# Hybrid encoder with a routed expert FFN: places from chosen ranks and filler products in the dispatch, own PSUM banks and ScalarE scaling in the last norm

## The reference

```
h = layer_norm(DEEPNORM_ALPHA * h + mix, ln1_g, ln1_b)
logits = h @ w_router + b_router
top_val, top_idx = top_k(logits, 4); gate = softmax(top_val)
# each expert's tokens are put into blocks, in the order of their rank in the expert
ffn[token] = sum over its 4 experts of gate * (clamped_swiglu(h @ w_e1[e] + b_e1[e]) @ w_e2[e] + b_e2[e])
out = layer_norm(DEEPNORM_ALPHA * h + ffn, ln2_g, ln2_b)
```

## Time and profile before

| | |
|---|---|
| time of three runs | 1649.32, 1646.13, 1648.8 us; median 1648.8 |
| the profiled execution | 1645.04 us, its span 1643.3 us, mean granted clock 0.975 |
| PE busy | 1505.0 us (92%) |
| DVE, ACT, POOL busy | 483.3, 249.8, 230.4 us |
| HBM read and written | 470.12 and 20.97 MB |
| chain that ended last, by engine | PE 72%, DMA 16%, SP's queue 5%, DVE 4% |

### The profile page before, as it was taken

The page is one execution under the profiler, slowest core; times in us unless marked ns, Lnnn a source line. Parts: engine busy times, 40 slices in busy tenths (PEclk is TensorE's granted clock), DMA queues, the critical chain, the costliest instruction groups (busy, mean ns, idle before and its releaser), DMA issues.

```text
span 1643.3 us, 30499 instructions
## 1 busy us (share of the span) xinstructions
PE 1505.0 (92%) x12438; PEld 689.1 (42%) x12439; DVE 483.3 (29%) x933; ACT 249.8 (15%) x302; POOL 230.4 (14%) x301
## 2 busy tenths in 40 slices
PE   7999999999999879999987788998799999999955
PEld 6744444444444534344433333343333444344422
DVE  5034343210004633223223223222322332222226
ACT  4011332110001121111101111011101101111112
POOL 1060000000000001211211211121121112111225
PEclk9999999999999879999999999999999999999987
DMA  5522100163305469999999999999999999999945
GB/s 188 182 77 86 36 1 0 45 191 90 90 1 205 185 258 414 416 414 416 416 414 416 416 414 416 416 416 415 416 416 414 417 416 415 405 374 418 414 187 219
DMA packets 136439, 474.31 MB, mean 289 GB/s; under 512 B 16732, under 2 KB 62532, under 8 KB 103384
## 3 DMA queue, kind: packets, MB, share of 16 engines
q1 hardware_dynamic: 123552, 445.10, 68.8%
q0 software_dynamic: 10896, 16.83, 2.8%
q10 hardware_dynamic: 1960, 11.94, 1.8%
HBM read 470.12 MB, written 20.97 MB: 299 GB/s over the span
## 4 chain that ended last, share of the span: by engine, by line
PE 72%; DMA 16%; SPq 5%; DVE 4%; issue 2%; ACT 1%; POOL 0%; POOLq 0%; DVEq 0%; ACTq 0%
PE ps L1456 26%; DMA big<-in_w_e 14%; PE ps L1489 12%; PE ps L1323 7%; PE ps L1244 5%; PE ps L1353 3%; PE ps L1381 3%; PE ps L1205 3%; PE ps L1337 3%; SPq L477 3%; PE ps L1331 1%; PE ps L1448 1%; SPq L460 1%; PE ps L1482 1%; PE ps L1272 1%
## 5 line engine op out<-in xcount | busy, mean ns | idle before, releaser
L1456 PE MATMUL ps<-big,rest 128*32 128x512 f32 x5040 | 568.9, 604 | 58.2 <-DMA big<-in_w_e 44.1
L1456 PEld LDWEIGHTS ps<-big,rest 128*32 128x32 f32 x5040 | 160.6, 111 | 429.7 <-issue 429.7
L1489 PE MATMUL ps<-big,rest 128*32 128x256 f32 x5120 | 287.9, 381 | 18.7 <-DMA big<-in_w_e 15.5
L1489 PEld LDWEIGHTS ps<-big,rest 128*32 128x32 f32 x5120 | 166.9, 110 | 130.2 <-issue 33.8
L1114 DVE TENSOR_TENSOR rest<-ps,rest 128x1024 f32<-128x1024 f32 x32 | 39.2, 1224 | 594.6 <-PE ps L1456 594.6
L605 POOL DMA_INDIRECT expert_rows<-rest,slot x128 | 127.2, 994 | 56.8 <-issue 29.3
L772 ACT ACTIVATE rest<-ps 128x1024 f32<-128x1024 f32 x33 | 68.6, 2079 | 434.5 <-PE ps L1448 434.5
L776 ACT ACTIVATE rest<-ps 128x1024 f32<-128x1024 f32 x32 | 32.7, 1023 | 426.8 <-PE ps L1482 296.4
L1244 PE MATMUL ps<-big,rest 128*128 128x512 f32 x192 | 82.8, 593 | 2.8 <-ACT big L650 2.8
L1133 DVE TENSOR_TENSOR rest<-ps,rest 128x1024 f32<-128x1024 f32 x32 | 39.2, 1224 | 129.6 <-PE ps L1489 129.6
L590 POOL COPY idx<-P 128x1 uint32 (+1 forms) x33 | 6.1, 183 | 488.5 <-PE ps L1448 469.2
(11 more groups left out here) (225 smaller groups left out, 1192.0 us busy)
## 6 DMA issues: line engine op xcount, KB each, us to landing
big<-in_w_e SPq DMA_DIRECT2D x379, 1024.0 KB
rest<-in_w_in SPq DMA_DIRECT2D x14, 1024.0 KB, 5.1
big<-expert_rows ACTq DMA_DIRECT2D x4, 2048.0 KB, 15.3
gate_area<-in_w_in SPq DMA_DIRECT2D x8, 512.0 KB, 5.3
rest<-in_w_in SPq DMA_DIRECT2D x8, 512.0 KB, 4.5
big<-in_w_out SPq DMA_DIRECT2D x1, 4096.0 KB, 13.1
X<-in_x SPq DMA_DIRECT2D x4, 512.0 KB, 9.4
gate_area<-in_w_branch_mlstm SPq DMA_DIRECT2D x4, 512.0 KB, 6.4
```

Of the source, the lines that this page charges most:

```text
L1456: last = mm(ps[TB * g:TB * (g + 1), b, :], xT[:, k, b, :], w1, start=(k == 0), stop=(k == KD - 1))
L1489: last = mm(ps[TB * g:TB * (g + 1), 4 + b // 2, YW * (b % 2):YW * (b % 2 + 1)], aT[:, b, k % 2, TB * (k // 2):TB * (k // 2 + 1)], W2[:, k ...
```

## The change

It touches two stretches, from the end of W_out to the first expert, and from the last expert to the end.

- `places`: instead of computing places for all 32 experts and picking four at the end (ten wide instructions and two reductions), DVE first picks the four chosen ranks from PSUM (one wide product, one reduction) and computes on 128x4 values. `iota_e` is replaced by the indices of the top four.
- The count reduction on DVE moves ahead of the wait for the slots; the index table is computed straight from PSUM, before `slots_f`; the number of further iterations comes from one conversion instead of a chain of comparisons.
- The first gather reads its indices from the table itself; POOL's copy to `idx` and the wait between go.
- `keep_clock(n)`: n products of the identity with itself into bank 4, whose result nobody reads, at six places on PE: 10, 4, 5, 3 and 14 before the first gather's rows are waited for, 5 before the first expert product.
- The first copy of `xT` is split: ACT takes bank 6, DVE bank 7.
- ACT loads the table with Ln and Exp once ahead of each norm.
- The loads of the combine are eight of 1 MB: rows 0 and 1 of a tile (`yg_front`), then rows 2 and 3 (`yg_back`). POOL takes row 0 in place of row 3. PE takes row 1 for both halves as soon as the front has landed, then rows 2 and 3. Each tile has two PSUM banks of its own.
- Last norm: DVE centres the tile before it refines its own 1/sqrt; ACT scales tile i-1 (`scaled`), DVE adds its bias. Tile 3 is scaled and biased on DVE as before.

```diff
@@ -582,13 +588,16 @@
-def gather(it, first=False):
-    if not first:
-        pool.wait_ge(x_tr, it)
-        own_wait()
+pool.indirect_dma_start(out=xg, out_offset=None, in_=x1_dram,
+                        in_offset=bass.IndirectOffsetOnAxis(ap=idx_table[:, 0:1], axis=0),
+                        bounds_check=S - 1, oob_is_err=False).then_inc(xg_landed, 16)
+def gather(it):
+    pool.wait_ge(x_tr, it)
+    own_wait()
...
-    pool.wait_ge(idx_ready, it + 1)
+    pool.wait_ge(idx_ready, it)
@@ -606,8 +615,6 @@
-gather(0, first=True)
-pool.wait_ge(x_tr, 1)
@@ -620,11 +627,16 @@
+def add_first(i):
+    pool.wait_ge(yg_front[i], 16)
+    row = yg[:, i, 0, :]
+    step(nc.gpsimd.tensor_scalar(row, row, gatew[:, TOPK * i:TOPK * i + 1], None, ALU.mult))
+    nc.gpsimd.tensor_tensor(X0v[:, i, :], X0v[:, i, :], row, ALU.add).then_inc(first_added, 1)
...
-    pool.wait_ge(yg_landed[i], 16)
-    row = yg[:, i, TOPK - 1, :]
-    step(nc.gpsimd.tensor_scalar(row, row, gatew[:, TOPK * i + TOPK - 1:TOPK * (i + 1)], None, ALU.mult))
-    nc.gpsimd.tensor_tensor(X0v[:, i, :], X0v[:, i, :], row, ALU.add).then_inc(fourth_added, 1)
+    add_first(i)
@@ -751,6 +763,7 @@
+act.preload_act_table_set("natural_log_exp_and_others")
@@ -787,10 +800,11 @@
+act.wait_ge(x_tr, 1)
+act.activation(xT[:, 0:KD // 2].rearrange("p c b t -> p c t b"), ps[:, 6, :].rearrange("p (c t b) -> p c t b", t=TB, b=NB), ACT.Copy).then_inc(xT_ready, 1)
...
-take_xT(1)
@@ -813,9 +827,17 @@
-    act.dma_start(yg[:, i], y_dram[P * i:P * (i + 1)]).then_inc(yg_landed[i], 16)
+    act.dma_start(yg[:, i, 0:2], y_dram[P * i:P * (i + 1), 0:2]).then_inc(yg_front[i], 16)
+    act.dma_start(yg[:, i, 2:4], y_dram[P * i:P * (i + 1), 2:4]).then_inc(yg_back[i], 16)
+act.preload_act_table_set("natural_log_exp_and_others")
...
-    rstd(NORM2 + i)
+    s0 = 16 * i
+    act.wait_ge(var2_ready, i + 1)
+    step(act.activation(stat[:, s0 + 14:s0 + 15], stat[:, s0 + 13:s0 + 14], ACT.Ln))
+    act.activation(stat[:, s0 + 14:s0 + 15], stat[:, s0 + 14:s0 + 15], ACT.Exp, scale=-0.5).then_inc(rstd2_ready, 1)
+    if i >= 1:
+        act.wait_ge(centred, i)
+        act.activation(X0v[:, i - 1, :], X0v[:, i - 1, :], ACT.Copy, scale=stat[:, s0 - 2:s0 - 1]).then_inc(scaled, 1)
@@ -1015,19 +1037,19 @@
-    rk, rt, ri = (v[:, E * i:E * (i + 1)] for v in (rank, rtmp, rint))
-    rp = ps[:, 7, E * i:E * (i + 1)]
-    step(nc.vector.tensor_scalar(ri, rp, 1.0 / TB, 0.5 / TB - 0.5, ALU.mult, ALU.add))
-    step(nc.vector.tensor_scalar(rt, ri, float(1 - NB * TB), None, ALU.mult))
-    step(nc.vector.scalar_tensor_tensor(out=rk, in0=rp, scalar=float(NB), in1=rt, op0=ALU.mult, op1=ALU.add))
-    nc.vector.tensor_scalar(ri, rp, 1.0 / CAP, 0.5 / CAP - 0.5, ALU.mult, ALU.add).then_inc(rank_read, 1)
+    rp = ps[:, 7, E * i:E * (i + 1)].rearrange("p (a e) -> p a e", a=1)
+    rk, rt = chosen_rank[:, TOPK * i:TOPK * (i + 1)], rank_tmp[:, TOPK * i:TOPK * (i + 1)]
+    pl, ri, ci = place[:, TOPK * i:TOPK * (i + 1)], rank_int[:, 0:TOPK], rank_int[:, TOPK:2 * TOPK]
+    nc.vector.tensor_tensor(chosen, oh[:, i], rp.broadcast_to([P, TOPK, E]), ALU.mult).then_inc(rank_read, 1)
...
-    step(nc.vector.tensor_copy(rt, ri))
-    step(nc.vector.scalar_tensor_tensor(out=rk, in0=rt, scalar=float(-NB), in1=rk, op0=ALU.mult, op1=ALU.add))
-    step(nc.vector.scalar_tensor_tensor(out=rt, in0=rt, scalar=float(E), in1=iota_e[:], op0=ALU.mult, op1=ALU.add))
-    for what, into in ((rk, place), (rt, itern)):
-        step(nc.vector.tensor_tensor(chosen, oh[:, i], what.rearrange("p (a e) -> p a e", a=1).broadcast_to([P, TOPK, E]), ALU.mult))
-        step(nc.vector.tensor_reduce(into[:, TOPK * i:TOPK * (i + 1)].rearrange("p (k a) -> p k a", a=1), chosen, X_AXIS, ALU.add))
+    step(nc.vector.tensor_reduce(rk.rearrange("p (k a) -> p k a", a=1), chosen, X_AXIS, ALU.add))
+    step(nc.vector.tensor_scalar(ri, rk, 1.0 / TB, 0.5 / TB - 0.5, ALU.mult, ALU.add))
+    step(nc.vector.tensor_scalar(ci, rk, 1.0 / CAP, 0.5 / CAP - 0.5, ALU.mult, ALU.add))
+    step(nc.vector.tensor_scalar(pl, ri, float(1 - NB * TB), None, ALU.mult))
+    step(nc.vector.tensor_copy(rt, ci))
+    step(nc.vector.scalar_tensor_tensor(out=pl, in0=rk, scalar=float(NB), in1=pl, op0=ALU.mult, op1=ALU.add))
+    step(nc.vector.scalar_tensor_tensor(out=itern[:, TOPK * i:TOPK * (i + 1)], in0=rt, scalar=float(E), in1=tf[:, i, :], op0=ALU.mult, op1=ALU.add))
+    step(nc.vector.scalar_tensor_tensor(out=pl, in0=rt, scalar=float(-NB), in1=pl, op0=ALU.mult, op1=ALU.add))
@@ -1059,24 +1081,19 @@
-dve.wait_ge(slots_done, 1)
-nc.vector.tensor_scalar(slots_f, ps[:, 2, 0:N_ITER], float(NO_TOKEN), None, ALU.add).then_inc(slots_read, 1)
-dve.wait_ge(slots_read, 1)
-nc.vector.tensor_scalar(idx_table[:, 0:N_ITER], slots_f, 1.0 / TOPK, -0.375, ALU.mult, ALU.add).then_inc(tables_ready, 1)
...
-step(nc.vector.memset(cnt[:, E + 1:E + 2], 0.0))
-for r in range(1, ROUNDS):
-    step(nc.vector.tensor_scalar(cnt[:, E + 2:E + 3], cnt[:, E:E + 1], float(CAP * r), float(E), ALU.is_gt, ALU.mult))
-    step(nc.vector.tensor_tensor(cnt[:, E + 1:E + 2], cnt[:, E + 1:E + 2], cnt[:, E + 2:E + 3], ALU.add))
+dve.wait_ge(slots_done, 1)
+nc.vector.tensor_scalar(idx_table[:, 0:N_ITER], ps[:, 2, 0:N_ITER], 1.0 / TOPK, NO_TOKEN / TOPK - 0.375, ALU.mult, ALU.add).then_inc(tables_ready, 1)
+nc.vector.tensor_scalar(slots_f, ps[:, 2, 0:N_ITER], float(NO_TOKEN), None, ALU.add).then_inc(slots_read, 1)
+step(nc.vector.tensor_scalar(more_iter[0:1, :], cnt[0:1, E:E + 1], 1.0 / CAP, 0.5 * (CAP - 1) / CAP - 1.0, ALU.mult, ALU.add))
...
-nc.vector.tensor_copy(more_iter[0:1, :], cnt[0:1, E + 1:E + 2]).then_inc(iter_ready, 1)
+nc.vector.tensor_scalar(more_iter[0:1, :], more_iter[0:1, :], float(E), None, ALU.mult).then_inc(iter_ready, 1)
@@ -1087,6 +1104,8 @@
+dve.wait_ge(x_tr, 1)
+nc.vector.tensor_copy(xT[:, KD // 2:KD].rearrange("p c b t -> p c t b"), ps[:, 7, :].rearrange("p (c t b) -> p c t b", t=TB, b=NB)).then_inc(xT_half, 1)
@@ -1154,20 +1173,45 @@
-for i in range(NT):
+def norm_2_statistics(i):
...
-    dve.wait_ge(fourth_added, i + 1)
+    s0 = 16 * i
+    dve.wait_ge(first_added, i + 1)
...
-        nc.vector.tensor_tensor(half, half, ps[:, 2 * (i % 2) + n, :], ALU.add).then_inc(combined_read, 1)
+        nc.vector.tensor_tensor(half, half, ps[:, 2 * i + n, :], ALU.add).then_inc(combined_read, 1)
...
-    close_statistics(NORM2 + i, D // BANK)
+    step(nc.vector.bn_aggr(stat[:, s0 + 12:s0 + 14], stat[:, s0:s0 + 12]))
+    nc.vector.tensor_scalar(stat[:, s0 + 13:s0 + 14], stat[:, s0 + 13:s0 + 14], LN_EPS, None, ALU.add).then_inc(var2_ready, 1)
+    layer_norm_center(NORM2 + i, t)
+def norm_2_root(i):
+    s0 = 16 * i
+    var, y, q = stat[:, s0 + 13:s0 + 14], stat[:, s0 + 14:s0 + 15], stat[:, s0 + 15:s0 + 16]
+    dve.wait_ge(rstd2_ready, i + 1)
+    step(nc.vector.scalar_tensor_tensor(out=q, in0=y, scalar=var, in1=y, op0=ALU.mult, op1=ALU.mult))
+    step(nc.vector.tensor_scalar(q, q, -0.5, 1.5, ALU.mult, ALU.add))
+    nc.vector.tensor_tensor(y, y, q, ALU.mult).then_inc(centred, 1)
+    return y
+def norm_2_bias(i):
+    dve.wait_ge(scaled, i + 1)
+    nc.vector.tensor_tensor(X0v[:, i, :], X0v[:, i, :], bias[:], ALU.add).then_inc(out_ready, 1)
+for i in range(NT):
+    norm_2_statistics(i)
+    y = norm_2_root(i)
...
-        layer_norm_scale(NORM2 + i - 1, X0v[:, i - 1, :], out_ready)
-    layer_norm_center(NORM2 + i, t)
-layer_norm_scale(NORM2 + NT - 1, X0v[:, NT - 1, :], out_ready)
+        norm_2_bias(i - 1)
+dve.wait_ge(centred, NT)
+nc.vector.scalar_tensor_tensor(out=X0v[:, NT - 1, :], in0=X0v[:, NT - 1, :], scalar=y, in1=bias[:],
+                               op0=ALU.mult, op1=ALU.add).then_inc(out_ready, 1)
@@ -1425,14 +1469,25 @@
+def keep_clock(n):
+    for _ in range(n):
+        mm(ps[:, 4, 0:P], ident[:], ident[:], start=True, stop=True)
+pe.wait_ge(wo_read, 2 * NT - 1)
+keep_clock(10)
...
+keep_clock(4)
...
+keep_clock(5)
...
+keep_clock(3)
@@ -1440,6 +1495,7 @@
+keep_clock(14)
@@ -1522,7 +1578,9 @@
+keep_clock(5)
...
+pe.wait_ge(xT_half, 1)
@@ -1550,13 +1608,14 @@
-    pe.wait_ge(yg_landed[i], 16)
+    pe.wait_ge(yg_front[i], 16)
...
-        if i >= 2:
-            pe.wait_ge(combined_read, 2 * (i - 2) + n + 1)
-        for k in range(TOPK - 1):
-            last = mm(ps[:, 2 * (i % 2) + n, :], gate_diag[:, TOPK * i + k, :], yg[:, i, k, BANK * n:BANK * (n + 1)],
-                      start=(k == 0), stop=(k == TOPK - 2))
+        mm(ps[:, 2 * i + n, :], gate_diag[:, TOPK * i + 1, :], yg[:, i, 1, BANK * n:BANK * (n + 1)], start=True, stop=False)
+    pe.wait_ge(yg_back[i], 16)
+    for n in range(D // BANK):
+        for k in range(2, TOPK):
+            last = mm(ps[:, 2 * i + n, :], gate_diag[:, TOPK * i + k, :], yg[:, i, k, BANK * n:BANK * (n + 1)],
+                      start=False, stop=(k == TOPK - 1))
...
```

(3 more changed lines are left out.)

11 lines of the change are left out of this document (8 added, 3 removed).

## The result

Five runs of the changed kernel took 1638.0 to 1640.26 us, median **1639.4**; before, run beside it, takes 1648.8 (1646.13 to 1650.06 in five runs). The ratio is 0.9942, with a 95% interval of 0.9930 to 0.9954. The forecast was 1637.0, range 1631.5 to 1643.0. The profiled execution took 1638.0 (span 1636.3) where that of before took 1645.04 (1643.3).

The account below looks back on a forecast made before the run. The prediction took the loop as bound by the weight stream over DMA, PE close behind, with serial ends. Dispatch 7.7 plus combine 4.1 gave 11.8 us off the median 1648.8: forecast 1637.0, range 1631.5 to 1643.

Parts of the forecast that it names:

- Terms 1 to 5: W_out to last slots: table loads 0.65, logits 1.75, ranks 0.9, places 0.8, last slots 0.4; done 4.5 us earlier.
- Term 6: From last slots to the gather's issue: one DVE instruction and POOL's issue, 0.85 us instead of 2.0, gain 1.1.
- Term 7: First gather meets the weight backlog: issued at 572.85, lands at 578.0, 4.1 us earlier than before.
- The rival in which the gather waits like the store: First gather takes 10.0 us, dispatch gives 2.8, total gain 6.9, time 1641.9; chance 0.10.
- The even share of the Trainium skill: Queues served in turn: the first gather gets half the rate, lands near 577.5, half a microsecond better.
- Term 8: Fillers before the first gather's rows: PE free at 577.3, rows come at 578.0, so they cost nothing.
- Term 9: After the gather: transposes 1.98 to 1.1 us, gain 0.9; split copy with five fillers, gain 1.05.
- Term 10: First expert product: 13.9 us at full clock instead of 15.54, gain 1.6; it ends 7.7 us earlier.
- The rival of the stream that swallows the dispatch: Expert loop: weights' volume alone sets its end, only the combine's 4.1 us stay, time 1644.7; chance 0.12.
- Combine, 4.1: Last expert to end: first half load lands 2.6 us earlier, last tile 0.5 shorter; gain 4.1 us (2.5 to 6).
- a combine without gain: Rival at the combine: POOL and DVE exclude each other, combine gains 0, total 7.7, time 1641.1; chance 0.10.
- the last rival: Dispatch: fillers don't hold the clock and queue at 1.2 GHz; 2.6 to 6.7 us slower, 1653.5; chance 0.08.

Follow-up runs that it names:

- no_fillers: Changed kernel without its 41 filler products on PE; median 1642.3 us, ratio 0.9956 to the kernel before.
- late_slice: Changed kernel with slice 7 of the second expert's weights loaded after slices 0 to 2, not before the gather; median 1637.8 us, ratio 0.9927 to the kernel before.
- tail_fillers: Changed kernel with 75 fillers ahead of the last half of the last expert's second product; median 1651.3 us, ratio 1.0016 to the kernel before.
- all_rests: Changed kernel with the last slice loaded later and fillers at 86 us, before the loop and before the last weights; median 1651.6 us, ratio 1.0016.
- fillers_alone: Kernel before with only the 41 fillers added at the same six places; median 1642.8 us, ratio 0.9966.
- loop_entry_fillers: Changed kernel with ten more fillers ahead of the expert loop; median 1635.8 us, ratio 0.9924 to the kernel before.
- late_slice_fillers: Changed kernel with the last weight slice loaded behind the others and ten fillers ahead of the loop; median 1636.0 us, ratio 0.9919 to the kernel before.
- early_fillers: Changed kernel with 20 fillers in TensorE's rest at 86 us; median 1640.1 us, ratio 0.9944 to the kernel before.
- whole_loads: Changed kernel with one 2 MB combine load per tile again instead of two halves; median 1641.9 us, ratio 0.9960 to the kernel before.
- combine_alone: Kernel before with only the change's combine and last norm; median 1644.3 us, ratio 0.9976.
- dispatch_alone: Kernel before with everything of the change up to the first expert, combine and last norm unchanged; median 1642.6 us, ratio 0.9962.
- scaling_on_dve: Changed kernel with ScalarE's last-norm scaling back on DVE, in one instruction with the bias; median 1638.3 us, ratio 0.9938 to the kernel before.

## Why the prediction was right, and where its sizes were off

**Terms 1 to 5, the slots done 4.5 us earlier.** Measured from W_out's last column it is 4.2: table loads 0.64 for 0.65, logits 1.65 for 1.75, ranks 0.84 for 0.9, places 0.81 for 0.8, last slots 0.3 for 0.4. In no_fillers logits and ranks take 3.63 and 1.92 as before, so those two hang on the fillers.

**Term 6, to the gather, 1.1.** It is 0.6; this step failed. I took 0.5 for what stands between DVE's instruction and the gather, near the 0.3 between two scatters. It is 1.00, of which 0.84 is POOL's issue. The nearer row is that of each gather in the loop, which waits for a copy on its own engine. In after's waits it reads (engine and line waited for, us, times, longest):

```profile
POOL rest L602 <- POOL idx L599: 27.1, 31, 0.9
```

I had read that time as the copy's. But the issue is as long with a copy ahead of it as without one, as the chain of waits of before shows just ahead of the gather:

```profile
577.63 0.85 issue
```

**Term 7, the gather lands 5.15 us after its issue.** 5.12. The reason is right, since late_slice has 3.5 with a slice less. That the number fits so well is luck. The gather was issued 18.0 us behind W_out's last column and not 17.2, so less backlog was left, and it brings 0.22 MB and not 0.5. The same sum with what the trace has, 1.47 MB of weights left at the issue and 0.22 of the gather at 0.42 MB/us, gives 4.0 (an estimate). What the sum left out is that a gather that meets nothing takes 3.5 to 3.6 as well, of which its bytes are 0.5. The slots' shortfall (0.3) and that of term 6 (0.5) came through, so the landing gained 3.3 and not 4.1. The rival in which the gather waits like the store (10 us) is out.

The even share of the Trainium skill (DMA: Bandwidth & Descriptors, "Queues, rings and completion order") would have given about 4.6 with the prediction's bytes. The trace doesn't agree with it: in the first 3.2 us 236 packets of weights moved and none of the gather's, where in before, with no backlog, its first packet came 2.0 us after the issue.

**Term 8, fillers before the rows cost nothing.** PE was free 1.62 us before they came. In late_slice they end just as the rows come, and with one more they would be on the path.

**Term 9, transposes and copy 1.95.** 1.46: the transposes gave 0.89 as said, but from their end to the product it is 1.82 and not 1.35. The two halves of the copy end 1.16 behind the transposes, the five fillers 1.12, and then PE's issue takes 0.70, where the 1.35 left 0.3. How much of that is the fillers' no_fillers tells, whose product starts 1.66 behind the transposes:

```profile
586.77 1.94 PE L1512 MATMUL ps<-big,rest 128*32 128x512 f32 x8 [1.66 <-ACT rest L804]
```

So the fillers cost 0.16 us there, and 0.3 of the shortfall is there without them. Product start: 4.7 earlier for 6.05.

**Term 10, first product 13.9, gain 1.6.** 13.98 and 1.56. Slice 7 didn't delay it.

Dispatch in sum: 6.3 for 7.7. **The loop** passed it on. It ends on the last weights, whose landing moved with the first product's end: 981.8 us behind it before, 982.3 after, 982.9 in late_slice. The 0.6 us that after loses is no loss that one can tell. Without tail_fillers and all_rests, from the end of the first product to DVE's last addition it is 985.2 to 985.5 us in the four kernels whose clock falls neither at the entry nor before the last 64 records (fillers_alone, loop_entry_fillers, late_slice_fillers, early_fillers), 986.4 to 986.9 in the three with the fall at the entry (before, after, whole_loads), 986.8 and 987.5 in the two with the late one (combine_alone, no_fillers) and 988.5 to 989.2 in the three with both (dispatch_alone, scaling_on_dve, late_slice). Short and long dispatches stand in the same groups. The rival of the stream that swallows the dispatch is out, for the late slice too.

**Combine, 4.1.** 4.3, with the right parts: loads in halves 2.8 (2.6 predicted), ScalarE's scaling nothing. That the sum is so near is luck in part: DVE's first tile starts 19.6 us behind its last addition of an expert's rows, 1.0 earlier than I laid out, and the distances between tiles add up to 20.3 and not 19.4, so two errors cancel. The first two distances grew to 6.8 and 7.4, not the 6.0 and 7.1 that I laid out; the last tile took 7.5 for 7.8. In the first of them DVE's centring starts at 1608.76, under POOL's addition of 1607.40, and lasts 2.07 us; the one at 1622.69, when POOL is done, lasts 1.27. By the rule of the Trainium skill (SBUF — State Buffer, "Who interferes with whom") a DVE instruction with two SBUF inputs waits while a POOL instruction that reads SBUF is under way, and the 2.07 agrees. In before DVE's scaling at 1623.07 kept its 1.28 wholly inside POOL's multiplication of 1621.91, so the rule doesn't fit every pair. Its whole consequence, a combine without gain, didn't come.

**The median.** From 1645.04 the terms as measured, 6.3 - 0.6 + 4.3, would give 1635.0; the profiled execution took 3.0 more for the fall at 88 us. My forecast of the median had no term for falls that come in one execution and not in the next. It doesn't need one for its own miss, though: 1648.8 less the same 10.0 is 1638.8 for 1639.4 measured, and of the 2.4 us between forecast and median 1.8 are the terms above.

**Clock.** It stayed at 1.00 through the whole dispatch, so the last rival is out, and that is what carried most: 4.7 of the 6.3 us.
